# A second, adding scatter per expert block, and four rows per token instead of eight in the last stage

## What is computed

```python
scores = jax.nn.sigmoid((t @ w_router).astype(jnp.float32))
_, idx = lax.top_k(scores + router_bias.astype(jnp.float32), TOP_K)      # TOP_K = 8
sel = jnp.take_along_axis(scores, idx, axis=-1)
gate_w = ROUTED_SCALE * sel / sel.sum(-1, keepdims=True)
...
def expert_block(args):                      # one block: up to 128 rows of one expert
    xblk, e = args
    g, u = jnp.split(xblk @ w_expert_gu[e], 2, axis=-1)
    return (jax.nn.silu(g) * u) @ w_expert_down[e]
...
routed = jax.ops.segment_sum(yb * row_w[:, None].astype(yb.dtype), row_tok, num_segments=n_tok)
...
return layer_norm_affine(DEEPNORM_ALPHA * stream + gate * y, ln_g, ln_b)   # y = routed + shared
```

## Time and profile before

| | |
|---|---|
| median of 3 runs | 2011.55 us (2010.14 to 2015.34) |
| profiled execution, its time | 2014.5 us |
| profiled execution, its span | 2012.7 us |
| mean granted TensorE clock | 0.967 |
| busy share of PE / DVE / ACT / POOL | 93% / 58% / 39% / 27% |
| bytes moved by DMA | 399.76 MB, of them 73.47 MB on q0 |

### The profile page before, as it was taken

How to read it: one execution, slowest core, us unless ns; L and a number is a source line. 1 busy time by engine, 2 the same in 40 slices (tenths; PEclk the granted TensorE clock), 3 DMA queues, 4 the chain that set the end, 5 groups by cost and what they waited for, 6 DMA issues and landing times.

```text
span 2012.7 us, 33743 instructions
## 1 busy us (share of the span) xinstructions
PE 1879.8 (93%) x7916; PEld 1332.3 (66%) x7917; DVE 1174.7 (58%) x1680; ACT 790.1 (39%) x1075; POOL 547.8 (27%) x680
## 2 busy tenths in 40 slices
PE   7999999997879999979999999999999999999686
PEld 1455458446754455468888888888888888888432
DVE  4743772203875553457548899563965892664186
ACT  0111110203230002147538788563865782665100
POOL 2000000003842231823333333332333332333200
PEclk9999996997999999989999999999999999999898
DMA  9732000001231334367657899762976893763696
GB/s 382 288 127 85 1 0 1 0 0 60 105 141 65 135 141 126 77 256 293 248 210 289 314 368 368 281 235 112 365 284 233 300 397 124 271 241 136 213 422 252
DMA packets 78543, 399.76 MB, mean 199 GB/s; under 512 B 21114, under 2 KB 21274, under 8 KB 57251
## 3 DMA queue, kind: packets, MB, share of 16 engines
q1 hardware_dynamic: 44736, 321.52, 41.6%
q0 software_dynamic: 32608, 73.47, 10.7%
q10 hardware_dynamic: 1156, 4.21, 0.5%
HBM read 374.05 MB, written 77.96 MB: 225 GB/s over the span
## 4 chain that ended last, share of the span: by engine, by line
PE 78%; DMA 7%; DVE 7%; POOL 2%; ACT 2%; issue 2%; SPq 1%; DVEq 0%; ACTq 0%; POOLq 0%
PE psum L1242 9%; PE psum L1244 9%; PE psum L1243 9%; PE psum L995 6%; PE psum L1229 5%; PE psum L1263 4%; PE psum L1261 4%; PE psum L1262 4%; PE psum L1004 3%; PE psum L1149 3%; PE psum L953 3%; PE psum L1034 3%; DMA arena<-pair_rows 3%; DMA arena<-in_toks 2%; PE psum L1303 2%
## 5 line engine op out<-in xcount | busy, mean ns | idle before, releaser
L1703 DVE TENSOR_TENSOR split_weights<-raw_weights,split_weights (+1 forms) x384 | 448.0, 1218 | 27.6 <-ACT split_weights L665 23.9
L665 ACT ACTIVATE split_weights<-raw_weights (+1 forms) x384 | 380.7, 1063 | 9.6 <-issue 8.6
L1242 PE MATMUL psum<-split_weights,split_rows 128*128 (+1 forms) x864 | 347.7, 402 | 0.0
L1244 PE MATMUL psum<-split_weights,split_rows 128*128 (+1 forms) x864 | 337.9, 391 | 0.0
L1243 PE MATMUL psum<-split_weights,split_rows 128*128 (+1 forms) x864 | 336.6, 390 | 0.0
L665 ACT ACTIVATE arena<-psum 128x1024 f32<-128x1024 f32 (+3 forms) x202 | 164.1, 820 | 418.1 <-PE psum L1132 128.2
L665 ACT ACTIVATE split_rows<-psum 128x256 fp32r<-128x256 f32 (+1 forms) x217 | 154.0, 710 | 161.1 <-PE psum L1250 150.5
L1244 PEld LDWEIGHTS psum<-split_weights,split_rows 128*128 128x128 f32 x864 | 162.3, 188 | 36.0
L1243 PEld LDWEIGHTS psum<-split_weights,split_rows 128*128 128x128 f32 x864 | 162.9, 189 | 31.0
L1242 PEld LDWEIGHTS psum<-split_weights,split_rows 128*128 128x128 f32 x864 | 163.1, 189 | 30.0
L1261 PE MATMUL psum<-split_weights,split_rows 128*128 x432 | 168.2, 389 | 2.0 <-ACT arena L665 2.0
(11 more groups left out here) (241 smaller groups left out, 2643.1 us busy)
## 6 DMA issues: line engine op xcount, KB each, us to landing
raw_weights<-in_w_gu SPq DMA_DIRECT2D x64, 2048.0 KB, 9.2
raw_weights<-in_w_dn SPq DMA_DIRECT2D x64, 1024.0 KB
arena<-pair_rows SPq DMA_DIRECT2D x32, 1024.0 KB, 21.3
arena<-in_w_ada SPq DMA_DIRECT2D x12, 2048.0 KB, 8.9
arena<-in_toks SPq DMA_DIRECT2D x18, 512.0 KB, 9.7
arena<-job_rows SPq DMA_DIRECT2D x16, 512.0 KB, 3.6
arena<-in_w_vog SPq DMA_DIRECT2D x1, 4160.0 KB, 13.0
arena<-in_w_qk SPq DMA_DIRECT2D x1, 4096.0 KB, 17.8
```

Source lines behind the costliest of these rows:

```text
L665: return act.activation(o, i, ACT.Copy)
L1242: mm(bank(3 + p), xk, part(par, 0, 512 * k), start=(k == 0), stop=False)
L1244: ins = mm(bank(3 + p), xl, part(par, 0, 512 * k), start=False, stop=(k == 7))
L1703: tt(cols(wsplit, (1 - par) * (2 * WE) + (WE + 1024 * c), 1024), cols(raw, (1 - par) * WE + 1024 * c, 1024), high, ALU.subtract).then_inc( ...
```

## The change

The results of a block are scattered twice. The index table `idxP` (8 x token + rank) is turned into `idxS`, two tables with rows 4 x token + (rank modulo 4): the first leaves all rows of ranks 0 to 3 out of bounds, the second those of ranks 4 to 7. Ranks count down from the highest expert, so the first scatter of a block writes the rows of a token's first four experts (ranks 4 to 7), and the second, an adding DMA, adds the rows of its later four. `pair_rows` has 4096 rows instead of 8192. The adding scatter waits until both scatters of the block before have landed.

```diff
+HALF = TOPK // 2
+NSUM = SEQ * HALF
...
-        ybuf = [at(A0 + 1024 * i, 1024) for i in range(24)]
+        ybuf = [at(A0 + 1024 * i, 1024) for i in range(4 * HALF)]
-        PE_RANKS = (4, 5, 6, 5, 6, 5, 6, 6)
...
-            sp.wait_ge(S("x1_sum"), 16 * NTX)
-            for j in range(NTX):
+            sp.wait_ge(S("x1_sum"), 16 * (NTX - 2))
+            for j in range(NTX - 2):
                 sp.dma_start(x1_in[j], x1_dram[P * j:P * j + P, :]).then_inc(S("rows2_in"), 16)
+            sp.wait_ge(S("x1_late_sum"), 32)
+            for j in (NTX - 2, NTX - 1):
+                sp.dma_start(x1_in[j], x1_dram[P * j:P * j + P, :]).then_inc(S("x1_late_in"), 16)
             sp.wait_ge(S("experts_done"), 1)
             def load_pairs(j):
-                if j >= 3:
-                    sp.wait_ge(S("ysum_pe"), j - 2)
-                    sp.wait_ge(S("ysum_read"), j - 2)
-                for k in range(0, TOPK, 2):
+                if j >= 4:
+                    sp.wait_ge(S("ysum_pe"), j - 3)
+                for k in range(0, HALF, 2):
...
-            def scatter(b, p, nth):
+            def scatter(b, p, nth, before):
                 pool.wait_ge(S("m_y"), b + 2)
...
-                pool.indirect_dma_start(out=y_dram[0:NPAIR, :], out_offset=bass.IndirectOffsetOnAxis(ap=idxs[:, p:p + 1], axis=0),
-                                        in_=yB[:, p], in_offset=None, bounds_check=NPAIR - 1, oob_is_err=False).then_inc(S(f"stored{p}"), 16)
+                pool.indirect_dma_start(out=y_dram[0:NSUM, :], out_offset=bass.IndirectOffsetOnAxis(ap=idxs[:, 2 * p:2 * p + 1], axis=0),
+                                        in_=yB[:, p], in_offset=None, bounds_check=NSUM - 1, oob_is_err=False).then_inc(S(f"stored{p}"), 16)
+                pool.wait_ge(S(f"stored{1 - p}"), before)
+                pool.sem_inc(S("passed"), 1)
+                pool.indirect_dma_start(out=y_dram[0:NSUM, :], out_offset=bass.IndirectOffsetOnAxis(ap=idxs[:, 2 * p + 1:2 * p + 2], axis=0),
+                                        in_=yB[:, p], in_offset=None, bounds_check=NSUM - 1, oob_is_err=False, compute_op=ALU.add).then_inc(S(f"stored{p}"), 16)
...
-                for k in range(PE_RANKS[j]):
-                    if k in (0, 4):
+                for k in range(HALF):
+                    if k % 2 == 0:
...
             link(tt(idxP[:, :], Ttmp[:, 0], Ttmp[:, 1], ALU.add))
+            rows, more = idxS[:, 0:P], idxS[:, P:2 * P]
+            link(ts(more, idxP[:, :], 1, 0xFFFC, ALU.logical_shift_right, ALU.bitwise_and))
+            link(ts(rows, idxP[:, :], HALF - 1, None, ALU.bitwise_and))
+            link(tt(rows, rows, more, ALU.bitwise_or))
+            link(ts(more, idxP[:, :], HALF, 11, ALU.bitwise_and, ALU.logical_shift_left))
+            link(tt(more, more, rows, ALU.bitwise_or))
+            link(ts(rows, more, NPAIR, None, ALU.bitwise_xor))
...
             for j in range(NTX):
                 y = yres[j]
-                b6, b7 = (ybuf[TOPK * (j % 3) + k] for k in (6, 7))
-                if PE_RANKS[j] == 4:
-                    dve.wait_ge(S(f"y_in{j % 3}1"), 16 * (j // 3 + 1))
-                    link(tt(y, ybuf[TOPK * (j % 3) + 4], ybuf[TOPK * (j % 3) + 5], ALU.add))
-                dve.wait_ge(S(f"y_in{j % 3}2"), 16 * (j // 3 + 1))
-                link(tt(b6, b6, b7, ALU.add))
-                if PE_RANKS[j] == 4:
-                    link(tt(b6, b6, y, ALU.add))
-                elif PE_RANKS[j] == 5:
-                    dve.wait_ge(S(f"y_in{j % 3}1"), 16 * (j // 3 + 1))
-                    link(tt(b6, b6, ybuf[TOPK * (j % 3) + 5], ALU.add))
+                dve.wait_ge(S("ysum_pe"), j + 1)
+                tt(y, psum[:, 0:1024] if j % 2 == 0 else psum[:, 1536:2560], g2B, ALU.mult).then_inc(S("ysum_read"), 1)
+                dve.wait_ge(S("ysum_read"), j + 1)
+                if j == NTX - 2:
+                    dve.wait_ge(S("x1_late_in"), 32)
+                link(stt(y, x1_in[j], ALPHA, y, ALU.mult, ALU.add))
+                moments(y, mv[:, 2 * j:2 * j + 2], "y_mv", hst[:, 8:20] if j % 2 else stats)
                 if j >= 1:
                     finish(j - 1)
-                dve.wait_ge(S("ysum_pe"), j + 1)
-                tt(y, psum[:, 0:1024] if j % 2 == 0 else psum[:, 1536:2560], b6, ALU.add).then_inc(S("ysum_read"), 1)
-                dve.wait_ge(S("ysum_read"), j + 1)
-                link(tt(y, y, g2B, ALU.mult))
-                link(stt(y, x1_in[j], ALPHA, y, ALU.mult, ALU.add))
-                moments(y, mv[:, 2 * j:2 * j + 2], "y_mv", hst[:, 8:20] if j % 2 else stats)
```

More of the change, by code:

```diff
@@ L146, in build @@
         idxg = sb("idxg", 2, U32)
-        idxs = sb("idxs", 2, U32)
+        idxs = sb("idxs", 4, U32)
         zrow = sb("zrow", P, parts=8)
@@ L255, in build @@
         idxP = sb("idxP", P, U32)
+        idxS = sb("idxS", 2 * P, U32)
         tbl = sb("tbl", 3 * P + 2, I32, parts=1)
@@ L290, in build @@
         shared_dram = nc.dram_tensor("shared_rows", [SEQ, D], F32, kind="Internal").ap()
-        y_dram = nc.dram_tensor("pair_rows", [NPAIR + NBUF, D], F32, kind="Internal").ap()
-        pairs = y_dram[0:NPAIR, :].rearrange("(t k) n -> t (k n)", k=TOPK)
+        y_dram = nc.dram_tensor("pair_rows", [NSUM + NBUF, D], F32, kind="Internal").ap()
+        pairs = y_dram[0:NSUM, :].rearrange("(t k) n -> t (k n)", k=HALF)
         grow = nc.dram_tensor("modulation_rows", [4, D], F32, kind="Internal").ap()
@@ L593, in add_shared @@
                 pool.wait_ge(S(f"x1_out{j % 2}"), 16 * 4)
-                pool.dma_start(x1_dram[P * j:P * j + P, :], shared_dram[P * j:P * j + P, :], accum_op=ALU.add, max_dma_last_dim=4 * D).then_inc(S("x1_sum"), 16)
+                pool.dma_start(x1_dram[P * j:P * j + P, :], shared_dram[P * j:P * j + P, :], accum_op=ALU.add, max_dma_last_dim=4 * D).then_inc(S("x1_sum" if j < NTX - 2 else "x1_late_sum"), 16)
             for j in range(3):
@@ L646, in _ @@
                     gather(bass.ds(2 * i + (p + 4), 1), p, 4 * i + (2 * p + 5))
-                    scatter(2 * i + p, p, 4 * i + (2 * p + 6))
+                    scatter(2 * i + p, p, 4 * i + (2 * p + 6), 32 * i + (16 + 32 * p))
             add_shared(6)
             add_shared(7)
-            scatter(2 * rest, 0, 4 * rest + 5)
-            scatter(2 * rest + 1, 1, 4 * rest + 6)
+            scatter(2 * rest, 0, 4 * rest + 5, 32 * rest + 16)
+            scatter(2 * rest + 1, 1, 4 * rest + 6, 32 * rest + 48)
             for p in range(2):
-                pool.wait_ge(S(f"stored{p}"), 16 * rest + 32)
+                pool.wait_ge(S(f"stored{p}"), 32 * rest + 48)
             for p in range(2):
@@ L850, in y_evac @@
                 act.wait_ge(S("block_done"), b + 2)
-                act.wait_ge(S(f"stored{p}"), 8 * (b - p) + 16)
+                act.wait_ge(S(f"stored{p}"), 16 * (b - p) + 16)
                 copy(yB[:, p], psY).then_inc(S("m_y"), 1)
@@ L1297, in combine @@
                     pe.wait_ge(S("ysum_read"), j - 1)
-                for k in range(PE_RANKS[j]):
-                    if k in (0, 4):
-                        pe.wait_ge(S(f"y_in{j % 3}{k // 4}"), (16 if k else 32) * (j // 3 + 1))
+                for k in range(HALF):
+                    if k % 2 == 0:
+                        pe.wait_ge(S(f"y_in{j % 4}{k // 2}"), 16 * (j // 4 + 1))
                     for h in range(2):
                         o = psum[:, (0 if j % 2 == 0 else 1536) + 512 * h:(512 if j % 2 == 0 else 2048) + 512 * h]
-                        ins = mm(o, ident, ybuf[TOPK * (j % 3) + k][:, 512 * h:512 * h + 512], start=(k == 0), stop=(k == PE_RANKS[j] - 1))
+                        ins = mm(o, ident, ybuf[HALF * (j % 4) + k][:, 512 * h:512 * h + 512], start=(k == 0), stop=(k == HALF - 1))
                 ins.then_inc(S("ysum_pe"), 1)
@@ L1741, in _ @@
             h_low(2 * rest + 1)
-            dve.wait_ge(S("rows2_in"), 48 + 16 * NTX)
+            dve.wait_ge(S("rows2_in"), 48 + 16 * (NTX - 2))
             def finish(i):
```

6 lines of the change are left out of this document (3 added, 3 removed).

## The result

The changed kernel is slower: median 2034.29 us (2023.38 to 2037.23, 9 runs) against 2014.73 us (2010.14 to 2016.85, 9 runs) for the kernel before in the same measurement, ratio 1.0086 with a 95% interval of 1.0071 to 1.0102. I had forecast 1999.5 us and faster; the range of 1973 to 2023 does not hold it, and it came out on the side of rival C. (The forecast took its 3 us for the median from three runs of the kernel before, 2011.55 us; nine runs gave 2014.73.) Its executions scatter over 14 us, more than those of before.

What follows compares the result with a forecast made beforehand. PE, busy 93%, was taken to bound the expert stage and full DMA engines the last stage. Profiled 2014.5 - 38 + 2 + 24 = 2002.5 us, less 3 for the median: 1999.5 us; range 1973 to 2023.

Steps and rivals of the forecast that it cites:

- rival C: Expert stage: in dense runs each block waits for the previous adding scatter, 10.9 us or more a step; 2023 us, chance 0.21.
- Part 3: Expert stage, POOL's queue and q0: one more adding DMA per block delays the gather behind it, costing 24 us.
- 30 blocks: Expert stage: spacings of at most 10 us between gate-and-up loads, in four long runs of 14, 6, 6 and 4.
- bounds 0 and 48: Expert-stage cost: 0 us if landings shrink with half the rows, 48 us where the landing stays just over 10.
- the run of 14: Expert stage: longest dense run of single-block experts, 14 load steps of 9.51 us; forecast 10.3 us a step.
- short runs: Expert stage: 16 short load spacings in ones to threes; 1.6 us of slack and the light block behind absorb the delay.
- The wait is the dearer part.: Expert stage: waiting for the previous block's adding scatter to land costs more than the bytes' 0.3 us per block.
- Part 1: Last stage: fewer rows to load and sum, DVE the bound at 6.7 us a tile; gives 38 us, bounds 31 and 41.
- Rival D: Last stage: PE at the low clock becomes the bound, 6 to 7 us less gain; 2006 us, no separate chance.
- Part 2: Before the first gather: six DVE operations on the index table cost 2 us.
- B: Expert stage: added scatters stay hidden, the gather's lost 1.9 us eats slack alone, length unchanged; 1975.5 us, chance 0.20.
- The rule of 2.0 us and the bytes: DMA landing: such a DMA takes about 2.0 us plus its bytes over 436 GB/s, so landings would never bind.

Runs made afterwards that it cites:

- e13: e4 plus, per block, a second plain scatter whose 128 indices are all out of bounds, so it moves no rows: 1998.9 us, ratio 0.9925.
- e7: e4 plus three small POOL operations behind each scatter, about 2 us and no DMA: 1983.7 us, ratio 0.9835.
- e1: Changed kernel without the adding scatter's wait for the landings of the block before: 2014.5 us, ratio 1.0007.
- e3: Changed kernel with its wait, second scatter writing plainly to a tensor never read (half the results left out): 1999.3 us, ratio 0.9916.
- e2: e1 with the second scatter writing plainly to a tensor never read (half the results left out): 1993.8 us, ratio 0.9898.
- e6: e4 plus, per block, an adding scatter whose 128 indices are all out of bounds, so it moves no rows: 2001.2 us, ratio 0.9928.
- e9: Changed kernel with one scatter per block that adds all rows into four per token, pair_rows cleared early, no wait: 2000.6 us, ratio 0.9936.
- e4: One plain scatter per block as before the change, with the changed last stage reading four of eight rows (half left out): 1978.8 us, ratio 0.9825.
- e8: Changed kernel with PE summing three of a token's four rows, all still loaded: 2027.3 us, ratio 1.0062.
- e5: e1 with the adding scatter moved one block later, behind the next gather, sum complete: 2004.0 us, ratio 0.9944.
- e12: One adding scatter per block into two rows per token, cleared early, no wait, moved behind the next gather: 1997.0 us, ratio 0.9913.

## Why the prediction was wrong

**The chain of waits, and where it goes.** Part of the reading held: the gather's slack is the margin, PE waits for the gather and not for weights, and it waits in single-block stretches or right behind them. The size of the loss was beyond rival C's.

**Part 3, "a step longer by 0.8 us over the 30 blocks ... 24 us", bounds 0 and 48.** This is the step that turned the sign. It measured 56.9 us of load span. The 30 spacings themselves lost 28.8 us, and the run of 14 came out at 10.39 us a step for a forecast 10.3, but that is luck: in that run eleven steps stayed as they were and three took 1.2, 4.6 and 6.2 us more. With these 28.8 us alone the change would have been some 5 us faster (33.7 in the last stage). The other 28 us lie where the prediction charged nothing, "In the short runs 12.7 - 1.9 - 9.2 = 1.6 us of slack and the light block behind take up the delay": 10.9 of them right behind the long runs, 17 in and behind the short ones. The median landing of 9.2 us hid this; a stall comes from a single long one (11.3 and 15.3 us above) on a queue that already runs late. Three prices were left out or mis-sized as well. First, I priced the third DMA by its bytes (0.3 us a block) and 1.9 us of POOL; e13 shows that it costs 20 us with no bytes, of which e7 leaves at most 5 to POOL's time. I had the packets in the text, and gave them no term. Secondly, I took the landing of a plain scatter in the dense stretch (10.0 us) for that of the adding one, and expected it to shrink; in e1, without the wait, it was up to 16.9 us. Thirdly, no term for the clock: PE's waits are followed by work at a lower clock, and that is 18 to 19 of the 57 us. The bound "48 us where the landing stays just over 10" was a chain of landings alone; with plain landings such a chain costs next to nothing (e3 against e2), so it bounded the wrong thing.

**"The wait is the dearer part."** Half right. It is worth 20 of the 55 us lost, no more than the adding itself, and only with it: with plain landings it costs nothing that can be told (e2, e3). That adding without rows is no dearer than plain without rows (e6, e13) and that adding with rows is 21 us dearer than plain with rows (e1, e2) puts this part on the rows: read, added and written in DRAM. Why 0.3 us a block of engine time, by the 5.8 us per MB that I had, makes 21 us over 108 blocks stays open: the engines stood at 0.98, so a delay of what stands behind is likely, but adding twice the rows cost no more than 22 us (e9).

**Part 1, "the last stage gives about 38 us back".** 33.7 in the two profiles, 36 by e4. The step that failed here: "PE needs 8 products a tile: 24 took 10.54 us at full clock, so 3.5 us". The third tile sums six ranks in two halves, 12 products, and the profile has two rows for each; a product takes 0.88 us, eight take 7.0, over DVE's 6.7. PE became the bound of the stage, with tiles of 6.86 us, as e8 shows by removing a quarter of it, 7.1 us. The first sum was read 14.8 us after the landing, forecast 12. Rival D named this bound, but through a low clock; the windows show 1.00 from 1970 us on, so that its price of 6 to 7 us came near the measured shortfall of 4.3 (33.7 for 38) is luck. The landing of the last scatter moved nothing noticeable to the stage: with lighter load it landed after 2.72 us instead of 6.60.

**Part 2, 2 us for six operations.** They took 1.7 us on DVE, 849.60 to 851.33, but what stands ahead of them ran 1.9 us earlier in this execution, and the first gather went out at 853.03 against 853.23. One execution each cannot tell whether they cost anything.

**Rivals.** B fell: even e1, without the wait, is 37 us longer in the expert stage. C was right in sign. Its sign in the profile, 10.9 us and more a step in the run of 14, did not come (10.39), its price was too low, and its mechanism, a chain of landings, is worth at most the 20 us of the wait.

**The rule of 2.0 us and the bytes** (the Trainium skill, "DMA: Bandwidth & Descriptors", section "Anatomy of one DMA — SWDGE (gpsimd) path"): the trace disagrees, the empty adding scatters of e6 landed after 7.5 us in the median. The other rule that the prediction took from the same page of the Trainium skill, turns between queues a packet at a time (section "Queues, rings and completion order"), fits e13, where packets without bytes cost some 15 us beyond POOL's time; no run here varied the number of packets of a DMA or the length of the weights' packets, so that it is this and nothing else stays open.

## What to carry to other kernels

Do not price a gather or scatter by its bytes where another queue keeps the DMA engines full: here a DMA per block that moved nothing, 144 packets, cost 20 us in 108 blocks. Look for that cost in a few large stalls and not in a longer step: a margin that is judged by median landings (9.2 us of 12.7) is used up by single ones of 11 to 15 us. In this stage each us of PE's waits came with half a us more of slower work. Moving a transfer behind the one that is urgent helps that one, but look at which buffer it then holds longer (e5, e12). If rows must be added in DRAM, clear the target in an idle stretch and let the one scatter that is there anyway do the adding, with rows far enough apart in time that no wait is needed: that was 1.1% faster than before, where the split in two was 0.9% slower.

## What was not expected of the hardware

- An indirect scatter whose rows are all skipped leaves 144 packets: 32608 packets on q0 without it (e7), 48160 with it (e13), for the same 73.5 MB.
- GpSimd is busy 1.54 to 2.64 us with an adding indirect DMA (median 1.59), against 1.02 us in the median with a plain one, whether or not any row is in bounds.
- Adding 8192 rows in place of writing them (e9 against e4) raised q0's share of the engines from 10.8% to 16.1% of the span.
- A product of 128 x 512 in float32 stands in the profile as two rows, 0.44 us each in sequence at full clock.
